# Folding the pooling's channel maps into w_out in a two-layer S5 and pooling trunk

## What is computed

```python
def pool_mixer(u, hist, start_pos, w_pool, scale):
    ...
    diff = pooled - u.astype(jnp.float32).reshape(bsz, L, POOL_GROUPS, POOL_GROUP_CH)
    y = jnp.einsum('blkc,kcd->blkd', diff, w_pool.astype(jnp.float32)).reshape(bsz, L, WIDTH_B)
    y = y * scale.astype(jnp.float32)
...
def trunk_layer(x, h0, pool_hist, start_pos, ...):
    hn = rmsnorm(x, g_mix)
    proj = hn @ w_in
    u_a = proj[..., :WIDTH_A]
    u_b = proj[..., WIDTH_A:]
    y_a, h_last = s5_mixer(u_a, h0, ...)
    y_b, new_hist = pool_mixer(u_b, pool_hist, start_pos, w_pool, pool_scale)
    x = x + jnp.concatenate([y_a, y_b], axis=-1) @ w_out
    hf = rmsnorm(x, g_ffn)
    x = x + jnp.square(jax.nn.relu(hf @ w_ff1)) @ w_ff2
```

## Time and profile before

| | us |
|---|---|
| median of 3 runs (range) | 2167.16 (2166.32 to 2168.86) |
| the profiled execution | 2165.3 |
| its span | 2163.5 |
| TensorE matmul busy | 2083.1 (96%) |
| VectorE busy | 1111.6 (51%) |
| ScalarE busy | 430.3 (20%) |
| mean granted clock of TensorE, as a share of 2.4 GHz | 0.992 |

### The profile page before, as it was taken

The page is one execution under the profiler, slowest core; times in us unless marked ns, Lnnn a source line. Parts: engine busy times, 40 slices in busy tenths (PEclk is TensorE's granted clock), DMA queues, the critical chain, the costliest instruction groups (busy, mean ns, idle before and its releaser), DMA issues.

```text
span 2163.5 us, 29153 instructions
## 1 busy us (share of the span) xinstructions
PE 2083.1 (96%) x12894; PEld 2043.6 (94%) x12894; DVE 1111.6 (51%) x1647; ACT 430.3 (20%) x507; POOL 151.5 (7%) x183
## 2 busy tenths in 40 slices
PE   6988799999999999999999999999999999999997
PEld 6878799999999999999989899999999999999997
DVE  7988556354635445353467845643333434343346
ACT  5221342121111111111231224311110101111112
POOL 0022021000000000000020310200000000000003
PEclk9999899999999999999999999999999999999999
DMA  3535311111122121122134461111111111111112
GB/s 151 153 88 157 93 39 64 42 47 40 49 81 69 41 68 54 49 67 107 74 108 132 105 199 40 37 52 40 49 40 49 40 49 41 48 42 46 47 42 83
DMA packets 68861, 152.64 MB, mean 71 GB/s; under 512 B 8288, under 2 KB 28544, under 8 KB 68352
## 3 DMA queue, kind: packets, MB, share of 16 engines
q1 hardware_dynamic: 47536, 105.95, 15.4%
q0 software_dynamic: 9392, 31.33, 4.6%
q10 hardware_dynamic: 11808, 13.51, 2.1%
HBM read 123.23 MB, written 27.53 MB: 70 GB/s over the span
## 4 chain that ended last, share of the span: by engine, by line
PE 82%; DVE 10%; ACT 3%; issue 2%; DMA 1%; POOL 1%; SPq 0%; DVEq 0%; ACTq 0%
PE tile L441 77%; PE tile L696 2%; DVE h_low L993 2%; DVE x L1338 2%; DVE w_low L989 1%; ACT h_high L745 1%; ACT w_high L730 1%; DVE dve_products_late L979 1%; POOL intra_weights L1569 1%; DMA w_raw<-w_blocks 1%; PE small L609 1%; PE small L603 1%; DVE pool_s L979 1%; PE small L494 1%; DVE states L979 0%
## 5 line engine op out<-in xcount | busy, mean ns | idle before, releaser
L441 PE MATMUL tile<-h_high,w_high 128*128 128x408 f32 (+1 forms) x1920 | 427.5, 331 | 23.0 <-DVE h_low L993 19.4
L1338 DVE TENSOR_TENSOR x<-tile,x 128x816 f32<-128x816 f32 (+1 forms) x304 | 205.8, 718 | 461.9 <-PE tile L441 447.8
L441 PE MATMUL tile<-h_high,w_low 128*128 128x408 f32 (+1 forms) x1920 | 422.7, 328 | 0.0
L441 PE MATMUL tile<-h_low,w_high 128*128 128x408 f32 (+1 forms) x1920 | 422.7, 328 | 0.0
L441 PEld LDWEIGHTS tile<-h_high,w_high 128*128 128x128 f32 x1920 | 320.8, 188 | 29.6 <-issue 18.6
L730 ACT ACTIVATE w_high<-w_raw 128x1024 fp32r<-128x1024 f32 x162 | 170.5, 1052 | 767.8 <-PE tile L441 749.7
L441 PEld LDWEIGHTS tile<-h_high,w_low 128*128 128x128 f32 x1920 | 320.2, 188 | 1.0
L441 PEld LDWEIGHTS tile<-h_low,w_high 128*128 128x128 f32 x1920 | 320.2, 188 | 1.0
L441 PE MATMUL tile<-hidden_high,w_high 128*128 128x408 f32 (+1 forms) x1440 | 318.4, 329 | 2.1 <-DVE x L1338 1.3
L441 PE MATMUL tile<-hidden_low,w_high 128*128 128x408 f32 (+1 forms) x1440 | 316.4, 328 | 0.0
L441 PE MATMUL tile<-hidden_high,w_low 128*128 128x408 f32 (+1 forms) x1440 | 316.4, 328 | 0.0
(11 more groups left out here) (192 smaller groups left out, 1681.1 us busy)
## 6 DMA issues: line engine op xcount, KB each, us to landing
w_raw<-w_blocks SPq DMA_DIRECT2D x164, 512.0 KB, 3.5
x<-x_t ACTq DMA_DIRECT2D x8, 544.0 KB, 11.5
u_blocks<-ua_dram SPq DMA_DIRECT2D x64, 68.0 KB, 2.8
x<-x_t POOLq DMA_DIRECT2D x8, 544.0 KB, 5.7
ya_dram<-u_blocks ACTq DMA_DIRECT2D x64, 68.0 KB, 2.2
y_a<-ya_dram POOLq DMA_DIRECT2D x8, 544.0 KB, 4.7
x_kept<-x ACTq DMA_DIRECT2D x8, 544.0 KB, 2.7
x<-x_kept POOLq DMA_DIRECT2D x8, 544.0 KB, 8.5
```

The source lines that it names most:

```text
L441: mm = pe.matmul(ps[tile][:, c, 0:(b - a) * J], lhs, xt[:, k, a * J:b * J], start=(first and n == 0), stop=(last and n == 2))
L1338: ins = v.tensor_tensor(xt, pt_, xt, ALU.add)
```

## The change

1. **The fold.** ScalarE and TensorE make the transposed, scaled maps once per layer: `mixes` transposes the four maps against an identity matrix (loaded by a DMA of its own) into a small bank and ScalarE writes them back with the scale. `fold(i)` multiplies each raw block of w_out's lower half (blocks 8 to 11) by them, in the two small banks; `split_hi` and `split_lo` of those blocks read the banks instead of the raw block. The four map tiles, `y_b_high` and `y_b` are gone; in their place `pooled_high` and `pooled_low` split the pooled frames themselves, which lie in SBUF, with the gaps between streams left out.
2. **Where folds stand.** `fold(0)` after w_in tile 6, `fold(1)` after tile 7, `fold(2)` after the first two half tiles, `fold(3)` after `wob(4)` in layer 0 and `wob(3)` in layer 1. Since the small banks are shared with `carry(q)`, each `carry` waits for `wlo_made` of the blocks folded before it.
3. **Half tiles.** `wob(0)` and `wob(1)` run interleaved, chunks 3, 2, 1 of both, then chunk 0 of both; GLU's first two the same way with chunk 3 last. The place of `carry(q)` among the half tiles is new in both layers.
4. **Scans.** ScalarE writes rows of decay factors (`decays`), with zeros where a row begins; VectorE adds the decayed initial state to one column and does one scan over 1096 elements per quarter in place of 16. `scan` now ends on a semaphore, for which `post` waits.
5. **VectorE's order** is new (below); the doublings of `rotations` do both halves in one operation; the two last operations of `pooled` are one.
6. **DMAs.** Chunks 0 to 5 of `x` are loaded by SyncE behind the fetch of block 11, once all `pooled_low` are done; chunks 6 and 7 by GpSimd also wait for all folds.

```diff
+                def fold(i):
+                    b = LB + B_WOB + i
+                    pe.wait_ge(raw_landed[b % 2], 16 * (b // 2 + 1))
+                    if i == 0:
+                        pe.wait_ge(mix_made, l + 1)
+                        pe.wait_ge(small_free, (SM["kernel", 0, 2, 1], SM["mix", 1])[l] + 1 + 2)
+                    else:
+                        pe.wait_ge(wlo_made, b)
+                    if i == 1 and l == 0:
+                        pe.wait_ge(small_free, SM["kernel", 0, 3, 1] + 1 + 2)
+                    block = raw[:, b % 2, :].rearrange("p (n k m) -> p k n m", n=2, k=KA)
+                    for k in range(KA):
+                        mm = pe.matmul(folded(raw[:, b % 2, :], k // 2)[0][:, k % 2], wp[:, k, :], block[:, k],
+                                       start=True, stop=True)
+                    mm.then_inc(fold_done, 1)
...
                 def carry(q):
...
+                    pe.wait_ge(wlo_made, LB + B_WOB + ((3, 4, 4, 4), (2, 3, 4, 4))[l][q])
                     pe.wait_ge(kin_in[q], 16 * BLK * (l + 1))
...
                 if l == 0:
-                    wob(0)
-                    wob(1)
+                    first_wobs()
+                    first_wobs_end()
+                    fold(2)
                     wob(2)
+                    wob(3)
                     carry(0)
+                    wob(4)
+                    pe.wait_ge(carry_free, 4)
+                    fold(3)
+                    wob(5)
+                    carry(1)
+                    wob(6)
+                    carry(2)
+                    wob(7)
+                    carry(3)
+                else:
+                    first_wobs()
+                    carry(0)
+                    first_wobs_end()
+                    pe.wait_ge(carry_free, GP + 4)
+                    fold(2)
+                    wob(2)
+                    carry(1)
                     wob(3)
+                    pe.wait_ge(carry_free, GP + 8)
+                    fold(3)
                     wob(4)
-                    carry(1)
+                    carry(2)
                     wob(5)
-                    carry(2)
                     carry(3)
                     wob(6)
                     wob(7)
...
+                block_at(LB + B_GLU)
+                for n in range(2):
+                    tile_at(LT + T_GLU + n)
+                    for k in range(KA - 1):
+                        if n == 0:
+                            pe.wait_ge(zlo_made, l * KA + k + 1)
+                        products(n, 0, KA * n + k, k, zhi, zlo, k == 0, False)
+                pe.wait_ge(zlo_made, l * KA + KA)
+                for n in range(2):
+                    products(n, 0, KA * n + KA - 1, KA - 1, zhi, zlo, False, True).then_inc(tile_done, 1)
...
                 for i in range(KA):
                     k = KA - 1 - i
-                    act.wait_ge(tile_done, LT + T_POOL + i + 1)
-                    for pt_, out in halves(ps[i % 2], ybh[:, k, :]):
-                        ins = act.activation(out, pt_, ACT.Copy, scale=lp[:, L_SCALE + k:L_SCALE + k + 1])
-                    ins.then_inc(ybh_made, 1)
+                    act.wait_ge(diff_made, l * KA + i + 1)
+                    for at_cols, frames in no_gaps(k):
+                        ins = act.activation(at_cols(dhi), frames, ACT.Copy)
+                    ins.then_inc(dhi_made, 1)
...
+                tt(w[:, g, :, JP], w[:, g, :, JP], begin[:, :, g].rearrange("p r g -> p g r"), ALU.add)
+                step.wait()
+                v.wait_ge(decay_made, 2 * (l * 4 + q + 1) + l + 1)
+                rows = w[:, g, :, :].rearrange("p g r j -> p (g r j)")
+                v.tensor_tensor_scan(rows, decay[:, :, :, :].rearrange("p g r j -> p (g r j)"),
+                                     rows, 0.0, ALU.mult, ALU.add).then_inc(scan_v, 1)
...
                     pre(0, 0, late)
+                    wob(0)
+                    wob(1)
                     scan(0, 0)
-                    wob(0)
+                    split_lo(10)
                     post(0, 0)
-                    wob(1)
                     pre(0, 1, late)
+                    wob(2)
                     scan(0, 1)
-                    wob(2)
+                    wob(3)
                     post(0, 1)
                     rotations(0, 3, late)
-                    wob(3)
                     pre(0, 2, late)
                     wob(4)
                     scan(0, 2)
+                    split_lo(11)
                     post(0, 2)
                     wob(5)
                     pre(0, 3, late)
```

260 lines of the change are left out of this document (173 added, 87 removed).

## The result

| | median of the runs | runs | profiled execution (span) |
|---|---|---|---|
| before | 2168.72 us | 2166.32 to 2169.86, 7 | 2165.3 us (2163.5) |
| changed | 2175.47 us | 2173.63 to 2178.10, 7 | 2174.66 us (2172.9) |

The ratio is 1.0036, 95% interval 1.0025 to 1.0047: slower by 5 to 10 us. The forecast was 2170.2, no change that can be told; the time lies inside the range, next to the slower rival's 2175. The forecast stood on a median before of 2167.16 (3 runs), which is 2168.72 now (7 runs): of the 5.3 us that it fell short, 1.6 are that shift and 3.7 the change (+6.8 instead of +3.0). Measured a second time, with other kernels on one chip, the changed kernel took 2175.10 (2174.18 to 2178.75, 5 runs), ratio 1.0039 (1.0025 to 1.0052).

What follows compares the result with a forecast made beforehand. VectorE's list was taken to bound layer 0's mixer and TensorE layer 1's. Layer 0 -2.6 and layer 1 +5.6 gave +3.0: 2165.3 becomes 2168.3, plus 1.9 to the median makes 2170.2 us; range 2162.5 to 2176.

Steps and rivals of the forecast that it cites:

- the slower rival: Both layers' new waits: the clock falls at each, three more cold starts, 4.7 us beside the forecast, 2175; chance 0.27.
- Layer 0, up to the states: Layer 0 from mixes to the first quarter's states: folds and x's load leave them at 184.9, as before (185.1).
- about 45.3 with small waits, 230.2: Layer 0, VectorE from first to last states: 45.3 us instead of 50.9, ending at 230.2 against 236.0.
- the forecast -2.6: Layer 0 as a whole: 2.6 us faster, 277.4 against 280.0 before.
- Behind it a cold carry 6.6: Layer 0, TensorE after waiting 6.2 us at carry(1): cold carry 6.6, then tiles and carries until 240.7.
- GLU: Layer 0 from the fourth z_low: 21.8 us, with the second half tile waiting 1.3 for wob(7)'s drain; layer 1: 1.0.
- x lands by 1250 ... crowded may cost 3 more: Layer 1, DMA order: adds nothing if x lands by 1250; crowded by the weights' loads, perhaps 3 us more.
- The other terms: Layer 1: mixes 0.5, folds 2.1 each, a wait of 4.2 before pooled work, 2.6 at carry(2).
- The clock falls at every new wait: Rival, both layers: three cold starts of 1.56 us beside the forecast, 4.7 us, 2175; chance 0.27.
- VectorE's saving reaches the end: Rival: block 11 split nearer wob(5), carries stay warm; layer 0 -8.6, layer 1 +3.5, 2162; chance 0.17.
- two cold starts: Slow-clock restarts inside the forecast: layer 0's cold carry(1) of 6.6 us, and 1.5 behind layer 1's 4.2 us wait.
- The change does no more than swap: Rival: fold equals maps in work; if the fold's split doesn't hold pooled_high, both mixers come out level, 2167; chance 0.11.

Runs made afterwards that it cites:

- e9: Changed kernel, in layer 0 ScalarE splits the GLU's first block ahead of writing carry(1) out instead of behind: 2171.81 us (1 run).
- e6: Changed kernel, layer 1's six x loads issued by GpSimd's queue between the carry weights of the second and third quarters: 2172.34 us (1 run).
- j1: Changed kernel with useless matmuls filling TensorE's new waits, no wait taken away: 2171.32 us (10 runs), ratio 1.0021.
- j2: Changed kernel with TensorE's new waits filled by useless matmuls, measured again beside the unchanged changed kernel: 2171.14 us (11 runs), ratio 1.0017.
- g1: The changed kernel again, nothing edited, for a second profile: 2177.52 us (1 run).
- g2: The changed kernel again, nothing edited, on one chip with the matmul-filled kernel: 2175.10 us (5 runs), ratio 1.0039.
- e3: Changed kernel, in layer 0 VectorE splits block 11 ahead of the third quarter's turn, a drain and a scan: 2170.79 us (1 run).
- f1: Changed kernel with earlier splits, pooled_high earlier, layer 1's x by GpSimd, GLU whole tiles in layer 1, early last drain in layer 0: 2152.88 us, ratio 0.9932.

## Why the prediction was wrong

**Layer 0, up to the states: right.** Tile 7 ended at 149.0 (149.4 said), VectorE stood 3.8 us for `pooled_high` (4.6), x's first drain was at 172.3 (173.2), 4.6 us after the issue (4.8), the first quarter's states at 183.7 (184.9), TensorE's wait at `carry(1)` 6.31 (6.2). The scan takes 2.44 us. The rows of before had given 2.1; the half throughput that the Trainium skill states ("DVE: opcode table, instruction layouts, handler registers and perf-mode slots", section "Datapath and trigger behaviour") had given an estimate of 2.4, and the trace sides with it. (I gave it with 1.13 ns an element; 1.22 us less 0.1 over 1024 elements is 1.09, and that is what gives 2.4.)

**Layer 0, "about 45.3 with small waits, 230.2": the step that failed.** I took the way from the first states to the last as VectorE's own work. The list has a split in it that needs ScalarE, and ScalarE's list had `carried(1)` ahead of it, late by the very wait that I had just worked out. I followed the 6.2 us down TensorE's queue and not down ScalarE's. The states were 6.6 us late. I would also have priced this at nothing, since TensorE was later still; e9, which moves only that split, shows that it costs 2.7 us or more, mostly through x's last chunks and the write of y. Without it layer 0 would stand at -2.3, next to the forecast -2.6. Counted by the terms of my sum, the miss is 1.5 by the end of the carries, 0.8 on the way of y (15.7 us instead of 14.9) and 0.5 in the GLU.

**"Behind it a cold carry 6.6": too small.** It took 7.9 until its last drain began, and with `carry(2)`'s second half waiting 1.25 for ScalarE the carries ended at 242.2 instead of 240.7.

**GLU: partly.** The order's delay by the bank was in the sum, and the trace has it (2.28 us). What I gave for the whole, 21.8 us, fell short by 0.5 in the profiled execution and by 2 in others, where the clock fell behind the wait for the bank; in layer 1 the 1.0 measured 1.4.

**Layer 1, "x lands by 1250 ... crowded may cost 3 more": the step that failed.** I had the condition and priced it outside the forecast. It was crowded: the carry weights filled the DMA engines as they had before, and x now went beside them on SyncE's queue instead of behind them on GpSimd's, landing in 12.2 us. I did not see which wait it would feed: `carry(1)`, through the split behind `pre(1, 3)`. 2.4 us and 1.4 of slow clock is 3.8; e6 gives 2.9 of it back. In the eight profiles that have this wait it lasts from 1.2 to 2.4 us, and the clock fell behind it in four, so its price differs from execution to execution. The other terms held: `mixes` 0.6, the folds 1.9 each (2.1 said), the waits 3.8 (4.2) and 2.71 (2.6).

**The rivals.** *The clock falls at every new wait* named the mechanism and 2175, and j1 and j2, 4 us faster, show it at work, though a part of the 4 isn't the clock's. Of its three further cold starts the first profile has one (7.73 us ahead of the GLU), g1 and g2 all three. But the one ahead of the GLU costs little, since TensorE waits there for the fourth z anyway, and the rest of the loss, x and ScalarE's late split, was in no rival's price. That its number came out is in part luck. *VectorE's saving reaches the end* is true of e3 and f1, and decided as said, by how early block 11 is split. I gave the forecast two cold starts and put the others with the rival, though the wait of 2.6 us at `carry(2)` was in my own sum. *The change does no more than swap* hung on `pooled_high` not being held by ScalarE's order: it was held (3.8 us in both layers).

What stays open: whether ScalarE's late copies in `carry(2)` (1.2 to 2.7 us in these kernels) can be avoided, and how the profiled executions' 9.4 us and the medians' 6.8 us divide; the clock's lottery moves single executions by 3 to 4 us, more than most of the terms here.
